# The experts' second product in unsplit float32, with 160 dense tokens instead of 192

## What is computed

```python
def peer(h, w_q, sub_keys, w_down, w_up):
    q = (ht @ w_q).reshape(T, PEER_HEADS, 2, PEER_HALF_DIM)          # 8 heads
    scores = jnp.einsum('thic,hikc->thik', q, sub_keys)
    sv, si = lax.top_k(scores, PEER_TOPK)                            # 16 of 128 keys, twice
    cand = sv[:, :, 0, :, None] + sv[:, :, 1, None, :]
    best, ci = lax.top_k(cand.reshape(...), PEER_TOPK)               # 16 of 256 pairs
    expert = (i1 * PEER_N_KEYS + i2).reshape(T, 128)                 # 128 experts a token
    gate = jax.nn.softmax(best, axis=-1)
    ...
        hid = gelu(einsum('cd,ckd->ck', xb, w_down[eb]))
        return einsum('ck,ckd->cd', gb * hid, w_up[eb])
```

## Time and profile before

| | |
|---|---|
| median of 3 runs | 1621.99 us |
| lowest, highest | 1620.65, 1622.55 us |
| the profiled execution | 1621.84 us, span 1620.1 us |
| TensorE's granted clock, mean | 0.993 |
| PE, DVE, ACT, POOL busy | 98%, 72%, 52%, 43% |
| DMA traffic | 472.64 MB, 292 GB/s over the span |

### The profile page before, as it was taken

How to read it: one execution, slowest core, us unless ns; L and a number is a source line. 1 busy time by engine, 2 the same in 40 slices (tenths; PEclk the granted TensorE clock), 3 DMA queues, 4 the chain that set the end, 5 groups by cost and what they waited for, 6 DMA issues and landing times.

```text
span 1620.1 us, 29114 instructions
## 1 busy us (share of the span) xinstructions
PE 1583.9 (98%) x9184; PEld 1440.4 (89%) x9184; DVE 1168.8 (72%) x3336; ACT 838.5 (52%) x1823; POOL 693.5 (43%) x568
## 2 busy tenths in 40 slices
PE   7989999999999999999999899999999999999997
PEld 5779999999999888888877899999999988888885
DVE  1720979758886899999823249794888769999995
ACT  5654241267773555555566532224777455555554
POOL 5566012356662334344177730243666514444430
PEclk9999999999999999999999999999999999999998
DMA  7346689979999899999754476998999989999992
GB/s 274 116 128 209 197 270 393 390 241 324 320 320 382 299 354 354 354 360 351 257 201 155 145 213 211 353 384 302 301 318 323 347 318 351 359 347 362 350 356 81
DMA packets 130906, 472.64 MB, mean 292 GB/s; under 512 B 15216, under 2 KB 15472, under 8 KB 130416
## 3 DMA queue, kind: packets, MB, share of 16 engines
q1 hardware_dynamic: 89328, 320.30, 56.1%
q0 software_dynamic: 41472, 151.01, 26.7%
HBM read 469.16 MB, written 1.05 MB: 290 GB/s over the span
## 4 chain that ended last, share of the span: by engine, by line
PE 96%; ACT 1%; DVE 1%; POOL 1%; issue 1%; DMA 0%; SPq 0%; DVEq 0%; POOLq 0%; ACTq 0%
PE ps L876 95%; PE ps L884 1%; POOL w_lo L503 1%; ACT arena L575 0%; DMA raw<-in_wm 0%; DVE xs L1277 0%; PE ps L1007 0%; DVE arena L1375 0%; DVE total L1232 0%; DVE arena L1251 0%; ACT hT_hi L600 0%; DVE hT_lo L1346 0%; ACT arena L634 0%; ACT w_hi L585 0%; ACT arena L648 0%
## 5 line engine op out<-in xcount | busy, mean ns | idle before, releaser
L876 PE MATMUL ps<-w_hi,hT_lo 128*128 128x512 f32 x1728 | 452.0, 394 | 0.0
L876 PEld LDWEIGHTS ps<-w_hi,hT_lo 128*128 128x128 f32 x1728 | 330.6, 191 | 70.4
L515 POOL DMA_INDIRECT arena<-in_wu,ret x128 | 207.1, 1618 | 358.2 <-DVE ps L1555 278.0
L876 PE MATMUL ps<-arena,raw 128*128 128x176 f32 x2048 | 317.4, 313 | 0.0
L876 PE MATMUL ps<-arena,w_raw 128*128 128x176 f32 x2048 | 316.9, 313 | 0.0
L876 PEld LDWEIGHTS ps<-arena,raw 128*128 128x128 f32 x2048 | 306.6, 190 | 1.0 <-issue 1.0
L876 PEld LDWEIGHTS ps<-arena,w_raw 128*128 128x128 f32 x2048 | 306.6, 190 | 0.2
L515 POOL DMA_INDIRECT arena<-in_rows,ret x160 | 170.1, 1063 | 275.4 <-ACT ret L771 142.4
L876 PE MATMUL ps<-w_lo,hT_lo 128*128 128x512 f32 x1024 | 279.0, 393 | 0.0
L503 POOL TENSOR_TENSOR w_lo<-raw,w_hi 128x1024 fp32r<-128x1024 f32 x80 | 193.3, 2423 | 118.2 <-ACT w_hi L585 68.3
L876 PEld LDWEIGHTS ps<-w_lo,hT_lo 128*128 128x128 f32 x1024 | 195.3, 191 | 42.0
(11 more groups left out here) (141 smaller groups left out, 1821.3 us busy)
## 6 DMA issues: line engine op xcount, KB each, us to landing
raw<-in_wd SPq DMA_DIRECT2D x128, 512.0 KB
w_raw<-in_wd SPq DMA_DIRECT2D x128, 512.0 KB
arena<-in_wu SPq DMA_DIRECT2D x128, 512.0 KB
raw<-in_wu SPq DMA_DIRECT2D x128, 512.0 KB
raw<-in_wm SPq DMA_DIRECT2D x80, 512.0 KB
arena<-in_rows,ret POOLq DMA_INDIRECT x160
arena<-in_subk SPq DMA_DIRECT2D x2, 1024.0 KB, 10.1
arena<-in_wu,ret POOLq DMA_INDIRECT x128
```

The source lines that it names most:

```text
L515: nc.gpsimd.indirect_dma_start(ring[:, s, :], None, table, bass.IndirectOffsetOnAxis(ap=index, axis=0)).then_inc(row_full[s], 16)
L876: return nc.tensor.matmul(out, lhsT, rhs, start=start, stop=stop, skip_group_check=shared)
```

## The change

The up stage's dense product is done in unsplit float32: each 128x128 chunk of a block is the stationary operand, and the hidden values of 160 tokens move, so the product comes out transposed (channels on partitions) in PSUM banks 4 to 7. At the end it is copied to SBUF (`upT`) and turned back. ACT's and DVE's split work of the up stage falls away. `HALFWAY` tokens are gone: 96 tokens (64 and `MORE = 32`) are now done by gathered rows in both stages, 96 gathers in each, and 160 are dense in both. The sums of the rows' products lie in SBUF (`sums`, `more_sums`), not PSUM. The ring has 10 slots in the down stage (5 gathers in flight at most) and 8 in the up stage; the up stage's blocks have 16 buffers, five of which are loaded as early as behind down block 15. The dots before the gates are 40 instead of 26, the gate groups 40 instead of 48, and they begin at block 79 instead of 68. The first picks go to POOL in four pieces, from block 18 on, not 25. The one-hots are shared out anew: POOL makes two tokens' scaled ones with one instruction each (`ALU.is_equal, ALU.mult`), DVE the other two's (256 columns instead of 512), ACT the unscaled ones of all four.

```diff
-HALFWAY = 16
-DENSE = SEQ - SPARSE
+MORE = 32
+DENSE_FROM = SPARSE + MORE
+DENSE = SEQ - DENSE_FROM
-RING = 5
-UP_RING = 4
-DOWN_RAW, UP_RAW = 8, 8
-ROWS = PICKS + HALFWAY
-GATHERS = ROWS + PICKS
+RING, IN_FLIGHT = 10, 5
+UP_RING = 8
+DOWN_RAW = 8
+ROWS = PICKS + MORE
+GATHERS = 2 * ROWS
-IDS_AT = 65
+IDS_AT = 76
-G_FROM = 68
+G_FROM = 79
-SPARSE_FIRST = 10
-EARLY, EARLY_PLACES = SPARSE_FIRST + HALFWAY, 14
+SPARSE_FIRST = 8
+EARLY, EARLY_PLACES = SPARSE_FIRST + MORE, 14
 def dots_after(b):
-    return EARLY + max(0, min(ROWS - EARLY, (b - G_FROM - 1) * (ROWS - EARLY) // 55))
+    return EARLY + max(0, min(ROWS - EARLY, (b - G_FROM - 1) * (ROWS - EARLY) // 47))
+UP_RAW = 16
+UP_BANKS = ((0, 1, 2), (3, 4), (5, 6), (7,))
+UP_EARLY, UP_EARLY_AT = 5, 2 * DOWN_RAW
...
+                blocks(sp, load_down_again, DOWN_RAW, UP_EARLY_AT, DOWN_RAW)
+                for j in range(UP_EARLY):
+                    load_up(j, j)
+                blocks(sp, load_down_again, UP_EARLY_AT, MORE_GATES_AT, DOWN_RAW)
...
                 sp.wait_ge(row_used, l * GATHERS + EARLY)
+                load_up(5, 5)
+                for j in (6, 7):
+                    sp.wait_ge(row_used, l * GATHERS + ROWS)
                     load_up(j, j)
+                for j in range(8, UP_RAW):
+                    sp.wait_ge(w_used, l * LAYER + UP_FROM - UP_RAW + j + 1)
                     load_up(j, j)
                 def load_up_again(b, j):
-                    sp.wait_ge(wlo_dve, l * BLOCKS + b - UP_RAW + 1)
+                    sp.wait_ge(w_used, l * LAYER + UP_FROM + b - UP_RAW + 1)
                     load_up(b, j)
...
                     if last is not None:
                         pool.wait_ge(row_used, last + 1)
+                    if IN_FLIGHT <= q < ROWS:
+                        slot, filled, _ = uses[q - IN_FLIGHT + l * GATHERS]
+                        pool.wait_ge(row_full[slot], 16 * (filled + 1))
...
-                def build_second(g):
+                def build_first(g):
                     if g > 1:
                         pool.wait_ge(g_mm, g - 1 + l * TGROUPS)
                     for k in range(POOL_TOK):
                         t = token_of(g) + k
-                        nc.gpsimd.tensor_scalar(oh2[:, g % 2, k, :], iota[:, :], i2T[:, t:t + 1], None,
-                                                ALU.is_equal).then_inc(oh2_done, 1)
+                        nc.gpsimd.tensor_scalar(oh1g[:, g % 2, k, :], iota[:, :], i1T[:, t:t + 1], gT[:, t:t + 1],
+                                                ALU.is_equal, ALU.mult).then_inc(oh1_pool, 1)
...
+                def up_bank(b, g, w, first=False, stop=False):
+                    for i, c in enumerate(UP_BANKS[g]):
+                        last = mm(up_psum(g)[:, i, :], w[:, c * P:(c + 1) * P], block_of(b), first and i == 0, stop,
+                                  shared=True)
                     return last
+                def up(b, j, first=False):
+                    pe.wait_ge(*up_arrival(b, j, l))
+                    for g in range(len(UP_BANKS)):
+                        last = up_bank(b, g, up_raw[j], first)
+                    last.then_inc(w_used, 1)
...
+                pe.wait_ge(row_used, (l + 1) * GATHERS)
+                for k in range(2):
+                    for of, part in ((sparse_to, sums), (more_to, more_sums)):
+                        mm(tile_psum(0, k), of, part[:, k * HALF:(k + 1) * HALF], of is sparse_to, False, shared=True)
+                def turn_back(g):
+                    pe.wait_ge(upT_done, l * len(UP_BANKS) + g + 1)
+                    for c in UP_BANKS[g]:
+                        k, o = c // (DC // 2), c % (DC // 2) * P
+                        last = nc.tensor.transpose(tile_psum(1, k)[:, o:o + P], upT[:, c, P:SEQ], ident[:, :])
...
+                        last = mm(tile_psum(0, k)[:, o:o + P], upT[:, c, 0:P], ident[:, :], False, o + P == HALF,
+                                  shared=True)
...
-                for b in range(2, BLOCKS):
-                    low_part(b, b % RAW)
-                    low_hidden(b, b % RAW)
-                    if b == 7:
-                        dve.wait_ge(hid_done, l + 1)
-                        step(nc.vector.tensor_tensor(row_coef, row_hid, row_gate, ALU.mult))
-                        settle()
-                    axpys(axpys_after(b - 1), axpys_after(b))
+                for n in range(ROWS):
+                    axpy(n)
```

547 lines of the change are left out of this document (258 added, 289 removed).

## The result

The changed kernel takes 1606.45 us (median of 4, 1605.1 to 1608.8) against 1622.24 before: ratio 0.9906, 95% interval 0.9889 to 0.9923, so 15.8 us or 0.97% faster. Forecast were 1586, 36 us faster. The time lies in the range of 1532 to 1630 but outside the sum's own bounds of 1560 to 1600; the sign is right, and 15.8 of the forecast 36 us are there.

A forecast was written before the change was run, and what follows sets the result against it. It took TensorE's instruction stream as the bound (PE busy 98%). Terms -52.0 - 14.2 - 34.0 + 7.1 - 0.8 + 11 + 4 + 43.4 = -35.5 against 1621.84 gave 1586 us, range 1532 to 1630.

The forecast's parts named there:

- TensorE's own stream: TensorE's work in both stages: blocks at 2.187 us, fewer gate groups, added transposes; alone it would give -93.9 us.
- two terms of DMA sharing: TensorE's waiting because block loads and gathers share transfers: +4 us for the down stages, +43.4 for the up stages.
- Turning back: Up stage's product: 8 transposes and 8 products a layer, 3.6 us, +7.1 for both; ACT's copies covered.
- Gate steps: Down stage: steps of 3.08 us, about 8 a layer with two dots 0.7 us late; +11, bounds 0 and 11.
- Down stage sharing: Early gathers slow block loads, lead just used up at block 76; 2 us a layer, +4, bounds 0 and 12.
- Up stage sharing: Gathers take half the transfers, TensorE starves from about 105 us; 21.7 us a layer, +43.4, bounds 14.7 to 26.6.
- Equal halves: Up stage: loads' and gathers' queues each get half while both have work; 1560 to 1605, chance 0.52.
- shares a little above half: Up stage: gathers take slightly more than half the transfers; 1605 to 1618, chance 0.06.
- Gathers under or over half: Up stage: gathers slower than half, 1530 to 1560, chance 0.19; or over 0.565, a loss, 1638 at 0.6, chance 0.09.
- The additions with both inputs in SBUF: Up stage: DVE's additions could stretch POOL's gather issue from 0.94 to 1.68 us, an argument for the faster 1543.
- A lower total: Up stage: transfers limited to 353 GB/s, TensorE loses 52.6 us instead of 21.7; 1648, chance 0.05.
- POOL's new instruction: Down stage: compare-and-multiply sets the pace at 0.80 us each, gain gone at 1.02, 1650 at 1.2; chance 0.05.

The follow-up runs named there:

- no_early_or_up_rows: Changed kernel without transfers of the 32 early second-kind gathers per down stage and last 88 per up stage, dots and additions still running: 1533.1 us.
- ring_of_4: Changed kernel with 4 ring slots instead of 8 for the up stage's rows: 1606.3 us.
- loads_first: Changed kernel with SyncE issuing loads of up blocks 8 to 15 before its wait for the down stage's last dot: 1589.4 us.
- one_dot: Changed kernel with late dots dealt one to each of 32 gate steps, the other 24 to the 15 steps behind the gates: 1608.4 us.

## Why the forecast was right in sign and wrong in size

**TensorE's own stream: right.** The prediction's sum without its two terms of DMA sharing is 1538.9. no_early_or_up_rows, which has only these two taken out, measured 1533.1. A down block took 2.173 us, not 2.187, and so did an up block, as forecast of the same form: over all 512 blocks that is 7.3 us, a little more than the whole difference of 5.8. Turning back ran without a wait.

**Gate steps: right.** Five steps took 16.22 us in layer 0, four of 3.07 and one 0.87 longer; six such and a shorter one at the end make 6 us a layer, 5.5 forecast.

**Down stage sharing: the first step that failed.** Put down were 2 us a layer; the trace has 23 blocks of about 2.56 instead of 2.17, 9.2 us too much, and taking the rows out gives 9.2 and 7.5. The rate was right (2.56 against 2.62). The lead was wrong. The working took 39 landed blocks at 236 us and even halves from there. But in the 8 us in which the second kind's gathers begin, the transfers were at 288 GB/s, with q1 at 1.11 MB where TensorE takes 1.93 (window 238 to 246 us):

```profile
DMA packets 807, 2.30 MB, mean 288 GB/s; under 512 B 253, under 2 KB 253, under 8 KB 805
```

With a difference of only 0.07 blocks a us between need and supply, each block of lead is 14 us of starving, six blocks. The forecast that the lead would just reach the gates at 332 us was 43 us off for three blocks. For both layers that is 16.7 us where the sum has +4 with bounds 0 and 12, so it lies outside them too.

**Up stage sharing: the term that decides, right in kind and too small, and the second step that failed.** Measured 29.3 us a layer, forecast 21.7, bounds 14.7 to 26.6, so it lies outside them. Equal halves, the end of the gathers (forecast 236 us into the stage, measured 238 to 241) and the full pace behind it came as described. What failed is the step "10 loads go out with the last dot of the down stage and the 8 first gathers have landed, so by 5.5 us about 11 blocks have landed". POOL issued 14 gathers between 487.4 and 507.9 us, so the ten loads, which SyncE issued from 495.8 on, shared with them from the first. The gathers' queue from 492 to 496 us, and the loads' queue from 496 to 500 and from 500 to 504:

```profile
q0 software_dynamic: 339, 1.25, 88.7%
...
q1 hardware_dynamic: 123, 0.48, 29.8%
...
q1 hardware_dynamic: 239, 0.88, 55.6%
```

By 504 us q1 had moved 1.36 MB, between two and three blocks where the forecast had five by 502. TensorE starved from 47 us into the stage, not 105. ring_of_4 is the check: there only four gathers can be out when the loads start, the stage starves from 97 us on, and its two up stages cost 22.5 and 22.1 us more than without the gathers, close to the forecast's 21.7. That SyncE holds back eight loads whose buffers are free was in the code and wasn't priced; loads_first shows it at 17 us. The prediction's own words for its 105 us don't fit it either: a lead of ten blocks at its difference of rates lasts 132 us, and 105 is what follows from the 21.7.

**The rivals.** By its number 1606.5 falls just outside equal halves (1560 to 1605) and into shares a little above half, which had a chance of 0.06; by its mechanism it doesn't. Gathers under or over half: neither, with 20.48 and 20.47 MB in 100 us. The additions with both inputs in SBUF did not slow the gathers: they were issued in 960 ns on average, against 1618 before. A lower total: it was 410 GB/s for 191 us, and the earlier trace rows was demand. The Trainium skill (HBM Reference, "Specifications (TRN2)") says that a core streaming alone measures well above its share of 358, about 425; the trace agrees with that and not with 358 as this core's limit. POOL's new instruction took 795 ns, just under the 0.80 at which it would have set the pace, and nobody waited for it.

**What was missing as a whole.** Each sharing term was priced by itself, but they are chained: any gain of TensorE in the down stage meets a date set by the last dot and 88 gathers at 2.56 us. one_dot shows that a down stage shorter by 3 us gains nothing. And the sum had no line for the whole: the up stage's 224 transfers need 224 x 1.28 = 287 us, less those that are through before it begins. The changed kernel spent 299, with a third of the rate unused in the last 70; paced and with early loads it took 279.

## What to carry to other kernels

When two queues share the transfers in halves, the one that an engine lives from gets half while the other has anything queued; so give the other its work by TensorE's progress, not as fast as its buffers come free. Price a lead in blocks at the very start of the sharing, and look at what an in-order queue holds back behind a wait that it doesn't need. Before a stage is shortened, ask which date ends the next one.
